# The delta net's gate product made as rows, and a weight piece split one round earlier

## The reference, cut to what matters

```python
proj = x @ w_in
dn_qkv, dn_ab, dn_gate, rk_in, rk_gate = jnp.split(proj, EVEN_SPLITS, axis=-1)
qkv = jax.nn.silu(dwconv_centred(dn_qkv, dn_conv)).astype(f32)     # 1536 columns, 5 taps
q, k, v = ...                                                      # q and k are then l2_normalized
ab = dn_ab.astype(f32).reshape(bsz, seq, 4, DN_HEADS)...           # 16 columns: the gates
g = -jnp.exp(dn_a_log) * jax.nn.softplus(ab[:2] + dn_dt_bias)      # decay of the state, two directions
beta = jax.nn.sigmoid(ab[2:])
```

## Time and profile before

| | us |
|---|---|
| median of three runs | 1719.74 |
| lowest and highest of them | 1704.57, 1719.89 |
| the profiled execution, whole | 1710.79 |
| its span of recorded instructions | 1709.5 |
| PE busy in the span | 1611.2 (94%) |
| DVE busy | 1124.0 (66%) |
| ACT busy | 778.0 (46%) |

### The profile page before, as it was taken

The page is one execution under the profiler, slowest core; times in us unless marked ns, Lnnn a source line. Parts: engine busy times, 40 slices in busy tenths (PEclk is TensorE's granted clock), DMA queues, the critical chain, the costliest instruction groups (busy, mean ns, idle before and its releaser), DMA issues.

```text
span 1709.5 us, 25042 instructions
## 1 busy us (share of the span) xinstructions
PE 1611.2 (94%) x10548; PEld 1414.6 (83%) x10548; DVE 1124.0 (66%) x1910; ACT 778.0 (46%) x1319; POOL 56.3 (3%) x52
## 2 busy tenths in 40 slices
PE   7998999999999989999999899889799899999897
PEld 6988888999889888888998889877699878885466
DVE  5586546555564865466555677754799878976676
ACT  4656344444454563445444455323322335645234
POOL 0000011000000000110000000100000000000000
PEclk9999999999999999999999989986999999999899
DMA  8553334556545533345555633100002056440042
GB/s 273 163 179 112 116 124 160 182 181 193 178 159 170 180 112 114 123 159 160 177 195 177 223 123 99 50 1 0 1 1 100 1 198 189 147 136 19 31 141 100
DMA packets 151185, 220.00 MB, mean 129 GB/s; under 512 B 6230, under 2 KB 110686, under 8 KB 150432
## 3 DMA queue, kind: packets, MB, share of 16 engines
q1 hardware_dynamic: 151072, 218.39, 39.9%
HBM read 217.31 MB, written 1.06 MB: 128 GB/s over the span
## 4 chain that ended last, share of the span: by engine, by line
PE 75%; DVE 15%; ACT 6%; DMA 2%; issue 1%; SPq 0%; DVEq 0%
PE bank L388 18%; PE bank L389 18%; PE bank L390 18%; DVE weights_low L364 4%; PE bank L2061 3%; PE bank L890 2%; PE bank L3398 2%; PE bank L2152 2%; ACT weights_high L351 2%; DVE place L2548 1%; PE bank L2354 1%; PE bank L3359 1%; PE bank L2118 1%; DMA place<-w_in_dram 1%; PE bank L3419 1%
## 5 line engine op out<-in xcount | busy, mean ns | idle before, releaser
L364 DVE TENSOR_TENSOR weights_low<-place,weights_high 128x1024 fp32r<-128x1024 f32 (+2 forms) x387 | 449.9, 1206 | 182.1 <-ACT weights_high L351 181.5
L351 ACT ACTIVATE weights_high<-place 128x1024 fp32r<-128x1024 f32 (+2 forms) x387 | 378.5, 1031 | 131.5 <-DMA place<-w_in_dram 39.1
L388 PE MATMUL bank<-hT_high,weights_high 128*128 128x256 f32 x1152 | 334.1, 290 | 3.7 <-DVE hT_low L485 2.7
L390 PE MATMUL bank<-hT_high,weights_low 128*128 128x256 f32 x1152 | 327.0, 284 | 0.0
L389 PE MATMUL bank<-hT_low,weights_high 128*128 128x256 f32 x1152 | 325.7, 283 | 0.0
L388 PEld LDWEIGHTS bank<-hT_high,weights_high 128*128 128x128 f32 x1152 | 219.2, 190 | 8.5 <-DVE hT_low L485 3.5
L389 PEld LDWEIGHTS bank<-hT_low,weights_high 128*128 128x128 f32 x1152 | 219.8, 191 | 0.6
L390 PEld LDWEIGHTS bank<-hT_high,weights_low 128*128 128x128 f32 x1152 | 218.5, 190 | 0.0
L389 PE MATMUL bank<-weights_low,branchT_high 128*128 128x512 f32 x256 | 101.8, 398 | 0.0
L388 PE MATMUL bank<-weights_high,branchT_high 128*128 128x512 f32 x256 | 101.3, 396 | 0.2
L390 PE MATMUL bank<-weights_high,branchT_low 128*128 128x512 f32 x256 | 100.5, 393 | 0.0
(11 more groups left out here) (429 smaller groups left out, 3350.7 us busy)
## 6 DMA issues: line engine op xcount, KB each, us to landing
place<-w_in_dram SPq DMA_DIRECT2D x48, 1024.0 KB, 5.3
place<-w_up_dram SPq DMA_DIRECT2D x32, 1024.0 KB, 5.6
place<-w_down_dram SPq DMA_DIRECT2D x32, 1024.0 KB, 4.9
place<-even_w_in_dram SPq DMA_DIRECT2D x17, 1024.0 KB, 5.2
place<-w_out_dram SPq DMA_DIRECT2D x16, 1024.0 KB, 5.0
place<-odd_w_in_dram SPq DMA_DIRECT2D x16, 1024.0 KB, 5.4
place<-w_branch_dram SPq DMA_DIRECT2D x12, 1024.0 KB, 5.0
place<-ple_gate_dram SPq DMA_DIRECT2D x8, 1024.0 KB, 5.1
```

Of the source, the lines that this page charges most:

```text
L351: nc.scalar.activation(high[:, lo:hi], self.raw[p % SLOTS][:, lo:hi], ACT.Copy).then_inc(*A("high", p, j))
L364: nc.vector.tensor_tensor(low[:, lo:hi], self.raw[p % SLOTS][:, lo:hi], high[:, lo:hi].bitcast(FP32), ALU.subtract).then_inc(*V())
L388: nc.tensor.matmul(out, left[0], right[0], start=first, stop=False)
L390: return nc.tensor.matmul(out, left[1], right[0], start=False, stop=last)
```

## The change

The 16 gate columns are made the other way round. `gates_tensor` keeps the weight piece as the stationary operand (128 x 16) and moves all 256 tokens through it, so that the result is 16 rows of 256 in one bank, `abT`, after 24 matmuls. ACT copies these 16 rows to `e.rhs`, and `gates_turned_tensor` turns them back with two PE transposes into the banks `("ab", 0)` and `("ab", 1)`. PE waits for ACT's copy (`("free", "abT")`) between its first silu step and the l2 sums of q. The sigmoid on ACT and the bias on DVE move behind the first step of the q normalization.

Beside it, round `(2, 0)` of the loop, the fifth, now splits two pieces, `ab` and `silu dn 0`. Round `(2, 2)` splits `silu dn 1`, and the split behind the loop goes. The number of calls in total is the same.

```diff
+def gates_tensor(k, e, ready):
+
+    T = k.T
+    b = k.claim("abT")
+    p, w = k.weights(("ab",), KT, DN_AB)
+    for kk in range(KT):
+        T.wait_ge(*ready(TT - 1, kk))
+        ins = k.product(b[0:DN_AB, 0:S], [part[:, kk, :] for part in w], [part[:, kk, :] for part in e.hT], kk == 0, kk == KT - 1)
+    ins.then_inc(*T("abT"))
+    T.same("used", p)
+
+def gates_turned_tensor(k, e):
+    nc, T = k.nc, k.T
+    for t in range(TT):
+        b = k.claim("ab", t)
+        T.wait_ge(("free", "abT"))
+        nc.tensor.transpose(b[:, 0:DN_AB], e.rhs[0:DN_AB, t * P:(t + 1) * P], k.table("ident")[0:DN_AB, 0:DN_AB]).then_inc(*T("ab", t))
...
@@ even_tensor @@
-    k.token_major(("ab",), [(("ab",), KT)], e.hT, DN_AB, h_ready)
+    gates_tensor(k, e, h_ready)
     squares = split(e.squares, 4, S)
-    for _ in l2_tensor(k, e, ("q",), squares, table("ones")[:, 0:1]):
+    for step, _ in enumerate(l2_tensor(k, e, ("q",), squares, table("ones")[:, 0:1])):
         fill()
+        if step == 0:
+            gates_turned_tensor(k, e)
...
@@ even_vector, in the loop @@
             k.low_of_next()
+            if (part, m0) == (2, 0):
+                k.low_of_next()
@@ even_vector, behind the loop @@
-    k.low_of_next()
-    delta_sums_vector(k, e)
-    for _ in l2_vector(k, e, ("q",), e.qkvT[:, 0], None, table("ones")[:, 0:1], P ** -0.5):
+    for step, _ in enumerate(l2_vector(k, e, ("q",), e.qkvT[:, 0], None, table("ones")[:, 0:1], P ** -0.5)):
         fill()
+        if step == 0:
+            delta_sums_vector(k, e)
...
@@ even_scalar, in the loop @@
             k.high_of_next()
+            if (part, m0) == (2, 0):
+                k.high_of_next()
@@ even_scalar, behind the loop @@
-    k.high_of_next()
-    A.wait_ge(("even_loaded",))
-    for t in range(TT):
-        A.wait_ge(("ab", t))
-        nc.scalar.activation(e.g_beta[:, 1, t, :], k.bank("ab", t)[:, 8:16], ACT.Sigmoid).then_inc(*A("beta_made", t))
-    for _ in l2_scalar(k, e, ("q",), 1):
+    A.wait_ge(("abT",))
+    nc.scalar.activation(e.rhs[0:DN_AB, 0:S], k.bank("abT")[0:DN_AB, 0:S], ACT.Copy).then_inc(*A("free", "abT"))
+    for step, _ in enumerate(l2_scalar(k, e, ("q",), 1)):
         fill()
+        if step == 0:
+            for t in range(TT):
+                A.wait_ge(("ab", t))
+                nc.scalar.activation(e.g_beta[:, 1, t, :], k.bank("ab", t)[:, 8:16], ACT.Sigmoid).then_inc(*A("beta_made", t))
```

## The result

| | us |
|---|---|
| before, 20 runs, median (lowest to highest) | 1709.22 (1700.4 to 1719.89) |
| after, 20 runs, median (lowest to highest) | 1717.6 (1714.69 to 1722.18) |
| ratio after to before, 95% interval | 1.0038 (1.0021 to 1.0054) |
| profiled execution after, whole and span | 1716.76, 1715.4 |

The changed kernel is slower by 0.38%, 6.5 us by the ratio, with 3.6 to 9.2 us inside the interval; the two medians lie 8.4 us apart. That is less than the 1% that the prediction set as its bound, but it is clear of zero. The forecast was 1720.5 us, 2.9 above the measured median. It was built on +4.8 us, which makes 1715.6 on the scale of the profiled execution, and that execution now took 1716.76.

What follows compares the result with a forecast made beforehand. The prediction took the ACT and PE branches meeting at `shifted 0` as the bound. Later start 1.5, slow transposes and sums 1.8, slow silu 1.5 made +4.8 us; between 1715.6 and 1724.5 it forecast 1720.5 us, range 1706 to 1730.

Steps and rivals of the forecast that it cites:

- Bound and mark: Start of `shifted 0` on PE at 1030.29 us, where ACT's and PE's branches meet; its shift is the end's shift.
- The loop: Fifth convolution round takes 7.94 us in place of 5.75, sixth stays at 7.74; ACT's last silu starts 2.19 us later.
- the repayment on ACT: Behind the loop ACT drops a split of 1.89 us and gains a copy of 0.42; with the longer loop +0.7 us.
- The copy and the stop: PE idles 8.7 us until ACT's copy ends at 1017.26; the l2 sums of q start 1.5 us later.
- The clock: PE at half clock behind the copy: 1.8 us for transposes and sums, 1.5 for silu matmuls (0 to 4.6).
- the 10.04 us wait: Earlier PE wait, followed by 16 fp32 records at 0.21 us each; taken as nearest to the 8.7 us stop.
- rival (a): Clock returns once PE has work, or the slow stretch at 1030.3 goes: +1.5 us or less, 1717 us; chance 0.2.
- (b): Second split in the fifth round almost free, last silu stays at 1014.12: -2.4 us, 1713 us; chance 0.1.
- the stretch at 1030.3: Half clock from 1030.3 to 1033.7 before the change, behind the l2 sums of k; absence worth up to 1.7 us.
- (c): Later half-clock stretches move, +-1.7 us each, three at most: +-5 us on top of the forecast; chance 0.15.
- three-run median of 1719.74: Median of the kernel before; with +4.8 us it gave 1724.5, the profiled execution 1715.6, the forecast lying between.
- From the stage to the end: Behind `shifted 0` engines run in fixed order, none waiting for a transfer, so the end shifts by the same amount.

Runs made afterwards that it cites:

- e2: Kernel before with only the second split moved into the fifth round and none behind the loop, gate columns as before; ratio 1.002 (1.0 to 1.0039).
- e1: Changed kernel with the gate rows kept but the pieces split where the kernel before splits them; ratio 1.0029 (1.0012 to 1.0047).

## Why the prediction was right

**Bound and mark.** That `shifted 0` is the point to watch, and that ACT and PE meet there, held in the changed kernel. Before, ACT's branch was one of ACT and DVE: the chain that the prediction reads as ACT alone from 1014.75 us has two splits of DVE in it, 2.36 us each, which changed no term of the sum. The point moved by 4.50 us in one profile and 5.70 in the other (35.36 against 29.66); 4.8 was forecast, and both lie within its bounds.

**The loop.** 7.94 us was forecast for the fifth round and 7.95 measured; the last silu 2.19 later, 2.20 measured. e2 confirms the repayment on ACT: +0.30 us.

**The copy and the stop.** The stop was forecast at 8.7 us and measured at 8.35 and 8.77. PE's wait ended 16.63 us behind the mark, to the hundredth where it was forecast (1017.26 - 1000.63), and that is luck in part. The copy took 0.27 us on the chain, not 0.42, nearer to the lower bound of 0.22, but the silu ahead of it took 0.63 there and not 0.53. The record of the copy is 0.36 us, between the 0.22 of 16 columns and the 0.58 of 512, so nothing here shows that its 16 partitions counted for anything. The transposes showed two records and not four, 0.33 us in place of 0.5. So the l2 sums started 1.84 us later than before, where 1.5 + 0.5 was forecast.

**The clock.** Half clock from the copy on held. For the transposes and sums I had put 1.8 us; the sums alone took 3.43 in place of 1.84, which is 1.6. For the silu steps 1.5 us, and the first profile has 1.56, the second more. The choice of the 10.04 us wait as the nearest row, and against rival (a), was the step that decided the size. It was weaker than it read: the 16 records behind that wait stand 0.21 us apart, but the granted clock in that stretch, 10.0 to 13.4 us, is 1.00 in the profile. The prediction took the spacing and did not look at the clock.

The Trainium skill, page "TensorE: Matmul & The Clock Gate", section "HAM oscillation — how this bites in real kernels", has the next burst start throttled where a burst of matmuls is shorter than the wait behind it. The trace doesn't test that rule for this stop: the wait took 8.35 us and the clock behind it was 0.50 in both profiles, but PE had worked without a wait for 19.7 us ahead of it in the first and for 11.6 in the second, so the burst was the longer one. The prediction drew more from the page than it says when it applied it to one long stop.

**The rivals.** (b), that the second split would be nearly free, fell with the round's 7.95 us. (a) fell by the clock's rows for the silu part, but its second half, that the stretch at 1030.3 goes, came true in the first profile and not in the second. The sum put that at up to 1.7 us; between the two kinds of profile it is 1.1 at the k tokens. (c), that slow stretches elsewhere move the time, is larger than I had it: I put up to 5 us, and one program's two profiles differ by 10 us behind the stage. That is also where the three-run median of 1719.74 came from. The 20-run median is 1709.22, so the profiled execution of 1710.79 was the typical one of that set, and placing the forecast halfway to the three-run median put it 3 us too high. Other sets of the same kernel have medians of 1709.48 to 1715.96, so a forecast of the absolute time could not have come nearer than that but by luck.

**From the stage to the end.** This step did not hold. The prediction took a shift of `shifted 0` as a shift of the end, since nothing behind it waited for a transfer, and called it a sign of being wrong if the stages after 1060 us ended by another amount. They did: from the mark to the end the first profiles differ by 7.7 us (716.6 against 708.9), with 4.50 at `shifted 0` and 3.43 at the k tokens. And the chain waits for two transfers there, `ple_gate` at 1392.79 for 5.19 us and again at 1661.19 for 7.05. The term was put at nothing; the 2.2 us of the first of them and the clock's stretches are what came in its place. That +4.8 us still lies inside the interval of the whole time is in part luck, as the 1.1 us won back at the k tokens and what was lost behind them work against each other.

**What stays open.** The ratio says 6.5 us (3.6 to 9.2), the stage says 4.5 to 5.7 at `shifted 0` and 3.4 to 5.7 at the k tokens. Both agree within the interval. e1 and e2 have ratios of 1.0029 and 1.002, some 5 and 3 us. Their stages cost 1.1 and 0.3 us at `shifted 0`; at the k tokens e1 costs nothing and e2 gains 0.8, because the half-clock stretch at `shifted 0` is missing in both. All profiles of the changed kernel and of the variants show one more half-clock stretch of 3.4 us or more, 91 to 98 us behind the mark, that neither profile of the kernel before shows. Whether that comes from where these few executions happened to stand or from the changed spacing isn't settled by single profiles.

## What to carry to other kernels

An engine that runs ahead of the others hides its slow work, so making that work cheaper gains nothing, and a new wait for the late engine takes the lead away. Before adding a copy between two steps of a leading engine, find where the copy stands in the other engine's list, and put behind the wait only what can't run before it: here one step number moved 4 us. Where the whole time spreads by more than the effect, a distance between two marks inside the trace settles what the runs can't, for the stage between them. What lies behind has to be looked at too: in the first pair of profiles 3.4 us were lost up to the k tokens and 4.3 behind them.

## What the runs showed of the hardware

The kernel before, profiled twice, had its stage alike to 0.01 us and its total 10 us apart. The clock stood at half for 71.7 us of the time from 1050 us on in one and for 92.2 in the other. TensorE's clock fell in places where PE was fully busy: at 1006.4 in the kernel before, amid matmuls that move 16 columns, and at 1019.7 in e1, behind 16 records of one column and three silu matmuls, with no wait of PE since 1011.59. It also fell inside PE's stops, at about 1009.0 in the first profile of the changed kernel, 1.9 us into the stop, and at about 1012.1 in the second, 5.0 us into it. Either stretch at 0.50 lasted 13.7 us, so the second ended later behind the stop, with 14 slow silu matmuls in place of 7. And the 24 matmuls with a stationary operand of only 16 columns and 256 moving ones kept their spacing of 0.12 us at a granted clock of 1.00.
